# Two matrix-vector products for a modulation: VectorE sums along the row with its accumulator output, in place of sums over partitions finished by TensorE

## What is computed

```python
def modulate(x, cond, norm_g, w_ada, b_ada):
    shift, scale, gate = jnp.split(jax.nn.silu(cond) @ w_ada + b_ada, 3, axis=-1)
    ...
    return rms_norm(x, norm_g) * (1 + scale) + shift, gate
```

## Time and profile before

| what | us |
|---|---|
| median of 3 runs (lowest, highest) | 1811.37 (1809.66, 1811.55) |
| the profiled execution | 1811.72 |
| its span, first to last instruction | 1810.1 |
| TensorE busy (98% of the span) | 1767.2 |
| VectorE busy (54%) | 970.7 |
| ScalarE busy (37%) | 676.6 |
| GpSimd busy (10%) | 188.0 |

### The profile page before, as it was taken

One profiled execution on the slowest core, in us unless ns is written; L12 is line 12 of the kernel. 1 busy time (PEld: TensorE's weight loads), 2 busy tenths in 40 slices (PEclk: granted clock), 3 DMA queues, 4 the chain that ended last, 5 costly groups with the idle time before them and its releaser, 6 DMA issues.

```text
span 1810.1 us, 22256 instructions
## 1 busy us (share of the span) xinstructions
PE 1767.2 (98%) x8184; PEld 1424.5 (79%) x8184; DVE 970.7 (54%) x1237; ACT 676.6 (37%) x945; POOL 188.0 (10%) x170
## 2 busy tenths in 40 slices
PE   8999999999899999999999999998999999999999
PEld 6888888877787777876888888874777777788887
DVE  4333358856773665455533333335969678754442
ACT  4322222235334455544322222225445544732321
POOL 0000001112312702011100000002110120000000
PEclk9999999989999999999999999999999999999999
DMA  5223246613121334212223223331222222133331
GB/s 203 93 93 103 94 159 203 206 48 123 47 70 59 115 104 165 94 47 93 94 93 103 94 95 103 105 101 38 89 91 91 93 78 93 58 119 114 100 105 64
DMA packets 50315, 182.68 MB, mean 101 GB/s; under 512 B 5648, under 2 KB 5904, under 8 KB 50000
## 3 DMA queue, kind: packets, MB, share of 16 engines
q1 hardware_dynamic: 44352, 161.50, 27.0%
q10 hardware_dynamic: 4896, 14.96, 2.5%
q0 software_dynamic: 1008, 5.41, 0.9%
HBM read 179.75 MB, written 2.10 MB: 100 GB/s over the span
## 4 chain that ended last, share of the span: by engine, by line
PE 89%; DVE 6%; ACT 2%; issue 2%; DMA 0%; DVEq 0%; ACTq 0%
PE proj L364 79%; PE aux L467 2%; DVE w_lo L356 1%; DVE y L1495 1%; PE aux L1341 1%; PE aux L1328 1%; PE aux L690 1%; ACT w_hi L349 1%; DVE a_lo L506 1%; PE aux L1133 1%; DVE h L502 1%; PE proj L1154 1%; PE aux L1318 0%; ACT md L812 0%; DVE score L771 0%
## 5 line engine op out<-in xcount | busy, mean ns | idle before, releaser
L356 DVE TENSOR_TENSOR w_lo<-raw,w_hi 128x1024 fp32r<-128x1024 f32 x304 | 405.5, 1335 | 452.9 <-ACT w_hi L349 445.9
L364 PE MATMUL proj<-a_hi,w_hi 128*128 128x512 f32 x1504 | 597.0, 397 | 16.2 <-DVE a_lo L1844 8.6
L364 PE MATMUL proj<-a_hi,w_lo 128*128 128x512 f32 x1504 | 588.6, 391 | 0.0
L364 PE MATMUL proj<-a_lo,w_hi 128*128 128x512 f32 x1504 | 588.4, 391 | 0.0
L349 ACT ACTIVATE w_hi<-raw 128x1024 fp32r<-128x1024 f32 x304 | 319.7, 1053 | 281.8 <-PE proj L364 244.1
L364 PEld LDWEIGHTS proj<-a_hi,w_hi 128*128 128x128 f32 x1504 | 284.3, 189 | 82.9 <-issue 21.5
L364 PEld LDWEIGHTS proj<-a_lo,w_hi 128*128 128x128 f32 x1504 | 284.4, 189 | 60.5 <-issue 2.6
L364 PEld LDWEIGHTS proj<-a_hi,w_lo 128*128 128x128 f32 x1504 | 283.9, 189 | 59.4
L364 PE MATMUL proj<-hid_hi,w_lo 128*128 128x512 f32 x352 | 139.0, 395 | 0.0
L364 PE MATMUL proj<-hid_hi,w_hi 128*128 128x512 f32 x352 | 139.0, 395 | 0.0
L364 PE MATMUL proj<-hid_lo,w_hi 128*128 128x512 f32 x352 | 139.0, 395 | 0.0
(11 more groups left out here) (295 smaller groups left out, 2012.7 us busy)
## 6 DMA issues: line engine op xcount, KB each, us to landing
raw<-stream SPq DMA_DIRECT2D x304, 512.0 KB, 3.4
ctxk<-ada_in ACTq DMA_DIRECT2D x12, 512.0 KB, 3.5
ctxv<-ada_in ACTq DMA_DIRECT2D x12, 512.0 KB, 3.6
h<-x_in SPq DMA_DIRECT2D x4, 512.0 KB, 6.8
out<-h ACTq DMA_DIRECT2D x8, 256.0 KB, 2.0
btab<-rpb_in POOLq DMA_DIRECT2D x4, 384.0 KB, 3.5
side<-mem_in POOLq DMA_DIRECT2D x1, 1024.0 KB, 5.1
side<-ctx_in POOLq DMA_DIRECT2D x1, 1024.0 KB, 7.9
```

The lines of the kernel that those rows point to most:

```text
L356: nc.vector.tensor_tensor(w_lo[:, st.slot], raw[:, st.slot], w_hi[:, st.slot].bitcast(F32), ALU.subtract).then_inc(lo_ready, 1)
L364: mm = nc.tensor.matmul(dst, a, b, start=start and n == 0, stop=stop and n == 2)
```

## The change

The matrix is laid out the other way round on the host: block a (of 24) has 128 outputs on partitions and the 1024 inputs along the row. The condition vectors come as one row of 2 x 1024, broadcast to all partitions (`cond_row`), and ScalarE does the Silu there. VectorE multiplies a block with a condition elementwise and its accumulator output gives the sum along the row, straight into one column of `modv`: two instructions for a block, 48 in all. The products go to `ada_prod`, which nobody reads. `pe_ada_turn` and `dve_ada_take` are gone; the bias is added in place behind the norm. `cond_row` and `ada_prod` fill all of `a_hi`'s place.

```diff
         with ExitStack() as ph:
-            ada_sums = sb("ada_sums", [P, 2, KD, T], F32, ph)
+            cond_row = sb("cond_row", [P, 2, D], F32, ph)
+            ada_prod = sb("ada_prod", [P, 2, D], F32, ph)
...
         def act_down_ada(act):
 
             act.dma_start(ada_w[0], ada_in[0]).then_inc(ada_load[0], 16)
+            act.wait_ge(strip_done, S_DOWN1)
+            act.dma_start(cond_row[:].rearrange("p c k -> p (c k)"), cond_in.partition_broadcast(P)).then_inc(in_cond, 16)
             for a in range(ADA_STRIPS):
                 split_hi(act, Nth(S_DOWN1 + a + 3))
+                if a == 0:
+                    act.wait_ge(in_cond, 16)
+                    nc.scalar.activation(cond_row[:], cond_row[:], ACT.Silu).then_inc(cond_silu, 1)
                 if a + 1 < ADA_STRIPS:
-                    ge(act, ada_step, 4 * a)
+                    ge(act, ada_step, 2 * a)
                     act.dma_start(ada_w[(a + 1) % 2], ada_in[a + 1]).then_inc(ada_load[(a + 1) % 2], 16)
 
         def dve_ada(dve, a):
 
             dve.wait_ge(ada_load[a % 2], 16 * (a // 2 + 1))
-            for kk in range(2):
-                k = 2 * (a % 4) + kk
-                w = ada_w[a % 2][:, kk * W5:(kk + 1) * W5]
-                for c in range(2):
-                    to = ada_sum(a // 4, c)
-                    if k == 0:
-                        nc.vector.tensor_scalar(to, w, cond_s[:, k, c:c + 1], None, ALU.mult).then_inc(ada_step, 1)
-                        continue
-                    dve.wait_ge(ada_step, 4 * a + 2 * kk + c - 1)
-                    nc.vector.scalar_tensor_tensor(to, w, cond_s[:, k, c:c + 1], to, ALU.mult,
-                                                   ALU.add).then_inc(ada_step, 1)
+            if a == 0:
+                dve.wait_ge(cond_silu, 1)
+            for c in range(2):
+                ge(dve, ada_step, 2 * a + c - 1)
+                nc.vector.scalar_tensor_tensor(ada_prod[:, c], ada_w[a % 2], 1.0, cond_row[:, c], ALU.mult, ALU.mult,
+                                               accum_out=modv[:, a, c:c + 1]).then_inc(ada_step, 1)
 
         def dve_down_ada(dve):
 
-            dve.wait_ge(strip_done, S_DOWN1)
-            dve.wait_ge(cond_silu, 1)
             for a in range(ADA_STRIPS):
...
-        def dve_ada_take(dve):
-            dve.wait_ge(ada_turned, 1)
-            nc.vector.tensor_tensor(modv[:], aux[:, 3, 0:6 * KD].rearrange("p (n t) -> p n t", t=2),
-                                    col("b_ada", 0, 3 * KD).unsqueeze(2).to_broadcast([P, 3 * KD, 2]),
-                                    ALU.add).then_inc(ada_out, 1)
+        def dve_ada_bias(dve):
+            dve.wait_ge(ada_step, 2 * ADA_STRIPS)
+            nc.vector.tensor_tensor(modv[:], modv[:], col("b_ada", 0, 3 * KD).unsqueeze(2).to_broadcast(
+                [P, 3 * KD, 2]), ALU.add).then_inc(ada_out, 1)
...
             act.wait_ge(lb_max, 2)
             nc.scalar.activation(lbv[:, 1:3], lbv[:, 1:3], ACT.Exp).then_inc(lb_exp, 1)
-            act.wait_ge(in_cols, 16)
-            nc.scalar.activation(cond_s[:].rearrange("p k t -> p (k t)"), col("cond", 0, 2 * KD),
-                                 ACT.Silu).then_inc(cond_silu, 1)
             act_ffn(act, S_FFN1, G_FFN1)
...
             dve_centre(dve, LN1)
-            dve_normalise(dve, LN1, 0, ADA_AT)
-            dve_ada_take(dve)
-            dve_normalise(dve, LN1, ADA_AT)
+            dve_normalise(dve, LN1)
+            dve_ada_bias(dve)
             dve_mix(dve, chain)
...
             pe_down(pe, S_DOWN1, G_DOWN1, 0)
-            pe_ada_turn(pe, 0, 4)
             pe_mean(pe, LN1)
-            pe_ada_turn(pe, 4, 12)
             pe_stats(pe, LN1)
-            pe_ada_turn(pe, 12, 6 * KD)
             pe.wait_ge(in_const, 16)
             pe_mix(pe)
```

More of the change, by code:

```diff
@@ L153, in leave, with hybrid_blocks @@
         self.extra = 0
[L156 removed]
+def hybrid_blocks(nc, stream, ada_in, cond_in, x_in, mem_in, ctx_in, cols_in, const_in, mask_in, rows_in, wst_in, band_in, rpb_in,
                   out):
@@ L280, in hybrid_blocks @@
         x_hi, x_lo = sem("x_hi"), sem("x_lo")
-        cond_silu = sem("cond_silu")
+        in_cond, cond_silu = sem("in_cond"), sem("cond_silu")
         hid_h, hid_l = sem("hid_h"), sem("hid_l")
@@ L289, in hybrid_blocks @@
         ada_load = [sem(f"ada_load{n}") for n in range(2)]
-        ada_step, ada_turned, ada_out = sem("ada_step"), sem("ada_turned"), sem("ada_out")
+        ada_step, ada_out = sem("ada_step"), sem("ada_out")
         mod_ready = sem("mod_ready")
@@ L682, in dve_down_ada @@
                                                    ALU.add).then_inc(proj_read[g.slot], 1)
-        def pe_ada_turn(pe, lo, hi):
-            for n in range(lo, hi):
-                fb, c = n // 2, n % 2
-                if n == 0:
-                    pe.wait_ge(ada_step, 4 * ADA_STRIPS)
-                mm = nc.tensor.matmul(aux[:, 3, n:n + 1], ada_sum(fb // 4, c)[:, fb % 4 * P:(fb % 4 + 1) * P],
-                                      ones_full[:, 0:1], start=True, stop=True)
-            if hi == 6 * KD:
-                mm.then_inc(ada_turned, 1)
-        def dve_ada_take(dve):
-            dve.wait_ge(ada_turned, 1)
-            nc.vector.tensor_tensor(modv[:], aux[:, 3, 0:6 * KD].rearrange("p (n t) -> p n t", t=2),
-                                    col("b_ada", 0, 3 * KD).unsqueeze(2).to_broadcast([P, 3 * KD, 2]),
-                                    ALU.add).then_inc(ada_out, 1)
+        def dve_ada_bias(dve):
+            dve.wait_ge(ada_step, 2 * ADA_STRIPS)
+            nc.vector.tensor_tensor(modv[:], modv[:], col("b_ada", 0, 3 * KD).unsqueeze(2).to_broadcast(
+                [P, 3 * KD, 2]), ALU.add).then_inc(ada_out, 1)
         def act_only_splits(act, s0, lo, hi):
@@ L2047, in weight_stream, with ada_rows @@
     return whole
-def ada_stream(i):
-    w_ada = i["w_ada_2"][0]
-    return np.concatenate([token_major(w_ada[:, n * W5:(n + 1) * W5]) for n in range(ADA_CHUNKS)], 0)
+def ada_rows(i):
+    return i["w_ada_2"][0].T.reshape(ADA_STRIPS, P, D)
 def column_table(i):
@@ L2114 @@
     arrays = {
-        "stream": weight_stream(i), "ada_in": ada_stream(i), "x_in": token_chunks(i["x"][0]), "mem_in": token_chunks(i["mem"][0]),
+        "stream": weight_stream(i), "ada_in": ada_rows(i), "cond_in": np.concatenate([i["c_2"].reshape(-1), i["c_ctx_2"].reshape(-1)]),
+        "x_in": token_chunks(i["x"][0]), "mem_in": token_chunks(i["mem"][0]),
         "ctx_in": token_chunks(i["ctx_2"][0]), "cols_in": column_table(i), "const_in": consts, "mask_in": masks,
```

9 lines of the change are left out of this document (1 added, 8 removed).

## The result

The change takes 1790.3 us, median of four runs (1789.78 to 1790.96), beside 1810.51 (1809.25 to 1811.55) for the kernel before: a ratio of 0.9889, 95% interval 0.9872 to 0.9906. That is 20.2 us less, where 10.1 were forecast. The profiled execution took 1789.94 us, its span is 1788.3.

What follows compares the result with a forecast made beforehand. The prediction took TensorE, busy for 98% of the span, to bound the kernel. Savings at LN1 of 1.2 + 8.9 = 10.1 us, off the median 1811.37, gave 1801.3 us, with the range 1799.3 to 1805.5.

Steps and rivals of the forecast that it cites:

- The sum: Whole kernel: 1.2 us ahead of LN1's squares plus 8.9 us behind them, 10.1 us less, giving 1801.3 us.
- At nothing: Effects outside the down projection and LN1 counted as zero: 16-column Silu, table load, 1 MB more moved, shorter SyncE loops.
- the slack: VectorE beside the first down projection: 72.5 us left for 24 modulation blocks, 3.02 us each, so nothing reaches LN1 late.
- Term A: LN1, column products ahead of mean and squares removed: last residual to first square product falls from 4.55 to 3.32 us, 1.23 us.
- Term B: LN1, column products behind the squares removed: TensorE starts the mix strips earlier by 8.9 us, bounds 8.7 and 9.25.
- The block: VectorE's modulation block beside the down projection: two accumulating instructions, 2.66 us against 2.65 before, bounds 2.28 and 2.94.
- The rival of half the rate: VectorE's accumulating instruction takes two cycles an element: block 4.56 us, LN1 36.9 us late, kernel 1838 us; chance 0.08.
- The condition row: ScalarE's 1024 KB broadcast takes 9.3 us, then Silu 1.91; VectorE's first block starts at 264 instead of 255.83, delay hidden.
- The limit of 267.8: Down projection: latest start of VectorE's first modulation block, 267.8 us, at which TensorE still needn't wait for strip 48.
- The clock: Start of the mix strips: same slow start at half clock, about 3.5 us, before and after, so no gain counted.
- rival 3: LN1: clock falls earlier, squares at 1.2 GHz or later recovery in the mix; 1803.3 us, up to 1806; chance 0.08.

Runs made afterwards that it cites:

- second trace of the old instructions: Kernel before with 128 unused bytes ahead of the FFN's hidden halves, giving it the places of the kernel after: 1798.84 us, ratio 0.9935.
- three copies: Kernel after with three copies over the whole condition row on ScalarE ahead of its Silu: 1789.82 us, ratio 0.9886.
- six: Kernel after with six copies over the whole condition row on ScalarE ahead of its Silu: 1797.47 us, ratio 0.9923.

## Why the prediction was right and wrong

**The sum was right in kind, and the forecast was wrong.** The measured 1790.3 lies outside the range of 1799.3 to 1805.5, because a term is missing. The terms that the 10.1 us are made of are found in the traces. At the old places the change takes 1801.28 us, but that this meets the 1801.3 so closely is luck: the kernel before had a median of 1809.79 beside it, where the forecast starts from 1811.37, and the difference of the medians is 8.5 us, not 10.1.

**The step that failed is the part "At nothing".** A term of 11.0 us was left at nothing there. The part goes through what the change takes away outside the two places, and names the Silu over 16 columns, the table load, the broadcast's bytes and SyncE's loops. It doesn't name what those 16 columns and their Silu result occupied. That they go moves every later tensor by 128 B, and with it some 1,700 products of 512 columns (1056 on `hid`, 192 on the mixer's result, 288 on y, 192 on m) from 0.2333 to 0.2267 us: 11.4 us by 0.0066 us each, and the move alone measured 11.0. The prediction read the earlier trace rows as "0.233 us each" and used it for the slack, and it took 0.233 as TensorE's pace. That the products on `a` go at 0.227 in the same trace, with the same shape and no wait in either, was there to be read and asked about, though not what it meant for this change: no row tells that places matter. The range, 2 us below the forecast and 4 above it, came from the terms and rivals that were listed. It could not cover one that was not.

**Term A, 1.23 us: right.** From the last residual to the first product with the squares are 3.31 us (370.57 to 373.88), forecast 3.32.

**Term B, 8.9 us: right in kind, and in size for the execution that it was read from.** From the first product with the squares to the first of the mix are 20.27 us before and 11.56 after, so B is 8.7 us, its lower bound. LN1's 10.2 us hold another 0.25, because the last block is shorter and the residual starts that much sooner. With the columns of the second trace of the old instructions (10.98 us in place of 12.89) B is 6.8. The prediction took the length of the columns as a constant; it changes by 1.9 us with the place where the low clock falls. TensorE starts the mix 0.90 us behind the start of the first low half, 0.15 behind its end, as forecast. Putting the 36 products back costs 8.0 us of the trace and 7.2 of the median, with another course of the clock. VectorE's bias, 0.20 us at 396.35, holds up nobody.

**The block: at its lower bound.** 2.66 us were taken, 2.28 to 2.29 are measured, that is twice 1.14: the accumulator costs nothing, since its read lies beside the next instruction. The rival of half the rate is out. The Trainium skill's rule for it, in "Vector Engine (DVE) Microarchitecture Reference", section "Points that are easy to get wrong", doesn't show here: with two f32 sources in SBUF and the accumulator output, 1.22 us are the same as the split of that shape without one. Its side of the argument holds: at 3.42 us a block the last residual is late by the 10.8 us that a slack of 3.0 gives.

**The condition row: earlier than assumed.** The broadcast of 1024 KB lands 7.2 us after its issue, not 9.3, so that 768 KB and 1024 KB take about the same; VectorE's first block starts at 261, not 264. The limit of 267.8 is right to a microsecond: three copies, with a start at 266.4, cost nothing, six, with a start at 273.3, a stop of 5.3 us.

**The clock: right in the kernel after, wrong in what it costs.** The squares run at full clock and the mix starts at 0.53 for 3.5 us. That slow start costs nothing after the change, as filling the idle time showed. But rival 3, which got 0.08, is what happened in the run with the columns put back, with 1.5 us as its price, and behind an idle time of 11.2 us, with 2.3.

## What to carry to other kernels

A change that drops or adds a tensor moves all that are laid out behind it; before a forecast, list which operands change their place, and after a result compare the time of one untouched product in both traces before looking for anything else. Where a kernel is bound by TensorE, weights and moving operands that lie alike modulo 256 B were worth 11 us of 1810 at one unused tensor's price, and up to 34 us were lost by placing them badly. To learn what a change itself does, run it with the old places as well. And a price that is read from one execution, with the clock as it fell there, carries that execution's luck: here 10.2 us in one trace and 8.4 in the next.

## What was not expected of the hardware

- The pace of a 128x512 product depends on where its operands lie against each other in a partition: 0.2267 us at the same place modulo 256 B, 0.2289 with the moving operand 64 B further on (the average of three kinds of product, one of which isn't slowed), 0.2333 at 128 and 192 B. Moving both changes nothing. Displacing `w_lo` alone slows the product that uses it and the one beside which it is loaded.
- VectorE's accumulator output is free in a chain of such instructions: 1.14 us from start to start for 1024 elements, the read of 0.08 us beside the next one.
- Two products of the same kind in one trace, without a wait, can differ by 3% for that reason alone (0.2333 and 0.227 before); the group means of the page show it (395 and 391 ns), and the starts show it better.
